# Conformer layer on eight cores: second half's normalized tokens transposed by DMA, W_out tiles re-placed in the down projection

## The reference

```
u = rms_norm(h, norm_mix_pre)
a_val, a_gate, q, k, v = split(u @ w_in)
conv_out = silu(layer_norm(depthwise_conv31(a_val * sigmoid(a_gate))))
attn_out = chunked_band_attention(q, k, v, rel_bias)
mixed = concat([conv_out, attn_out]) @ w_out
h = h + rms_norm(mixed, norm_mix_post)
u = rms_norm(h, norm_ffn_pre)
f = depthwise_conv3(u @ w_up);  gate, val = split(f)
h = h + rms_norm((gelu(gate) * val) @ w_down, norm_ffn_post)
```

## Time and profile before

| | |
|---|---|
| time, median of 3 runs (840.32 to 842.19) | 841.18 us |
| the profiled execution's own time | 841.79 us |
| its span on the slowest core | 840.7 us |
| spans of the eight cores | 834.7 to 840.7 us |
| mean granted TensorE clock of the cores | 0.987 to 0.996 of full speed |
| busy share of TensorE, VectorE, ScalarE, GpSimd | 94%, 70%, 59%, 21% |

### The profile page before, as it was taken

How to read it: one execution, slowest core, us unless ns; L and a number is a source line. 1 busy time by engine, 2 the same in 40 slices (tenths; PEclk the granted TensorE clock), 3 DMA queues, 4 the chain that set the end, 5 groups by cost and what they waited for, 6 DMA issues and landing times.

```text
span 840.7 us, 15580 instructions; the slowest of 8 cores (834.7 to 840.7 us)
## 1 busy us (share of the span) xinstructions
PE 790.6 (94%) x5324; PEld 420.1 (50%) x5324; DVE 588.2 (70%) x758; ACT 499.9 (59%) x764; POOL 179.7 (21%) x324
## 2 busy tenths in 40 slices
PE   1998998899998897999999999999999999999997
PEld 1545465554554445666666654444444444444443
DVE  2566477778757888889999984454488888885223
ACT  4567363525555787789888784323377777772111
POOL 3122121000003453232333311111222222200010
PEclk9999999999999999999999999999999999999999
DMA  8994778021637843599999995443398888811222
GB/s 258 310 292 133 126 151 101 27 44 9 127 92 129 166 157 102 60 101 107 111 113 114 181 147 159 153 161 139 126 153 78 78 76 80 77 15 50 102 101 101
DMA packets 145619, 101.00 MB, mean 120 GB/s; under 512 B 117122, under 2 KB 124674, under 8 KB 145156
## 3 DMA queue, kind: packets, MB, share of 16 engines
q0 software_dynamic: 95520, 31.37, 36.7%
q1 hardware_dynamic: 49444, 68.29, 27.8%
q10 hardware_dynamic: 576, 0.34, 0.1%
HBM read 110.31 MB, written 23.12 MB: 159 GB/s over the span
## 4 chain that ended last, share of the span: by engine, by line
PE 73%; DVE 13%; issue 7%; ACT 5%; DMA 1%; POOL 1%; DVEq 0%; ACTq 0%; POOLq 0%
PE ps L1277 24%; PE ps L1172 14%; PE ps L686 7%; PE ps L1088 5%; DVE big L1299 4%; DVE big L1302 4%; PE ps L672 3%; PE ps L599 3%; PE ps L658 3%; PE ps L920 2%; PE ps L790 2%; PE ps L826 2%; PE ps L615 1%; PE ps L1204 1%; PE ps L561 1%
## 5 line engine op out<-in xcount | busy, mean ns | idle before, releaser
L1277 PE MATMUL ps<-big 128*128 128x344 bf16 (+2 forms) x1760 | 310.9, 337 | 1.1 <-ACT big L1298 0.9
L1277 PEld LDWEIGHTS ps<-big 128*128 128x128 bf16 x1760 | 171.2, 98 | 139.8 <-issue 3.9
L1172 PE MATMUL ps<-big 128*128 128x512 bf16 x660 | 144.2, 378 | 0.0
L1299 DVE SCALAR_TENSOR_TENSOR big<-big 128x1026 f32<-128x1026 f32 (+1 forms) x88 | 113.0, 1285 | 20.3 <-ACT big L1289 11.2
L1163 POOL DMA_DIRECT2D big<-w_up x88 | 77.4, 880 | 213.0 <-PE ps L1277 192.4
L1302 DVE SCALAR_TENSOR_TENSOR big<-big 128x1026 f32<-128x1026 f32 (+1 forms) x88 | 113.3, 1288 | 9.4 <-DVE big L1299 0.7
L1294 ACT ACTIVATE big<-ps,big 128x1026 f32<-128x1026 f32 (+1 forms) x88 | 106.8, 1214 | 0.0
L1172 PEld LDWEIGHTS ps<-big 128*128 128x128 bf16 x660 | 63.7, 97 | 76.6
L801 ACT ACTIVATE big<-ps 128x1024 bf16<-128x1024 f32 x80 | 80.2, 1024 | 26.9 <-PE ps L790 22.3
L1088 PE MATMUL ps<-big 128*128 128x512 bf16 (+1 forms) x272 | 64.9, 391 | 2.1 <-DVE big L1036 2.1
L1290 ACT COPY big<-ps 128x1024 f32<-128x1024 f32 x44 | 44.6, 1015 | 36.1 <-PE ps L1277 36.0
(11 more groups left out here) (126 smaller groups left out, 934.2 us busy)
## 6 DMA issues: line engine op xcount, KB each, us to landing
big<-w_up POOLq DMA_DIRECT2D x88, 256.0 KB, 5.4
big<-xw SPq DMA_DIRECT2D x37, 512.0 KB, 6.6
big<-w_in SPq DMA_DIRECT2D x40, 256.0 KB, 12.3
h1s<-big SPq DMA_DIRECT2D x16, 512.0 KB, 2.9
big<-h1s SPq DMA_DIRECT2D x16, 512.0 KB, 5.1
out<-big SPq DMA_DIRECT2D x15, 512.0 KB, 2.9
big<-w_down POOLq DMA_DIRECT2D x22, 256.0 KB, 6.1
hd<-big SPq DMA_DIRECT2D x4, 512.0 KB, 3.4
```

The costliest lines, as they stand in the source:

```text
L1172: S.mm(lambda f=f, half=half, i=i: pe.matmul((PH[2] if i % 2 else PD).ap[:, half, :], lhsT=actb[f].ap[:, i * 128:(i + 1) * 128], rhs=Wd[f] ...
L1277: S.mm(lambda k=k, t=t, c0=c0, n_=n_: pe.matmul(pu.ap[:, t, 0:n_], lhsT=wb.ap[:, k, :], rhs=u2T.ap[:, k, c0:c0 + n_], start=(k == 0), stop ...
L1299: S.op("dve", lambda: dve.scalar_tensor_tensor(out=tbv, in0=xv[1], scalar=fdw.ap[:, cbk, 1:2], in1=tav, op0=ALU.mult, op1=ALU.add), reads= ...
```

## The change

For tiles 9 to 16 `wo_tp` no longer uses TensorE and ScalarE. The tile `ub5` is stored to a buffer in DRAM (`u5d`, 256 KB), and a second DMA from the SP queue, a transposing one (`dma_start_transpose`), reads it back into `u2q[t]`, laid out tile by tile as [8 channel blocks, 128 tokens]. Both are 8 instructions. The up projection of H = 1 reads its 512 columns as four runs of 128, one from each tile's buffer.

The down matmuls of each i are recorded in two equal pieces of 22, so there are 16 places p. The W_out tiles 9 to 16 go to the places `WPOS`, ahead of the piece there: two of three places for tiles 9 to 14, and the last two at places 9 and 10. `wo_u` and the store to `u5d` are recorded at the place after the tile's, the transposing DMA at the place after that. The eight `turns` are split over places 0 and 1.

A third edit is in `proj_a`: for group 4 and column blocks 0 and 1 (`pq`) the matmuls read their moving operand in the order q, s, that is 512 elements of 2 bytes with a step of 16 bytes, so that the sum lies in PSUM in that order and L694 reads both operands contiguously.

```diff
+WPOS = (0, 1, 3, 4, 6, 7, 9, 10)
...
+    u5d = nc.dram_tensor("u5d", [8, 128, D], BF16).ap()
...
+        u2q = [sb("u2q%d" % i, 16736 + i * 2048, [8, 128], BF16) for i in range(8)]
+        u2v = big[:, 16736 // 4:(16736 + 16384) // 4].bitcast(BF16).rearrange("p (t k m) -> p t k m", t=8, k=8)
...
+            pq = g == 4 and c < 2
             for k in range(8):
-                S.mm(lambda k=k: pe.matmul(b.ap[:, :n], lhsT=Wa.ap[:, k, col:col + 128], rhs=ut.ap[:, k, n0:N],
+                r_ = ut.ap[:, k, n0:N].rearrange("p (s q) -> p q s", q=8) if pq else ut.ap[:, k, n0:N]
+                S.mm(lambda k=k, r_=r_: pe.matmul(b.ap[:, :n].rearrange("p (q s) -> p q s", q=8) if pq else b.ap[:, :n],
+                                                  lhsT=Wa.ap[:, k, col:col + 128], rhs=r_,
...
-                    out=hs.ap[:, :, c, 0:s_], in0=sg.ap[:, :n].rearrange("p (s q) -> p q s", q=8), scalar=1.0,
-                    in1=b.ap[:, :n].rearrange("p (s q) -> p q s", q=8), op0=ALU.add, op1=ALU.mult),
+                    out=hs.ap[:, :, c, 0:s_], in0=v_(sg.ap[:, :n]), scalar=1.0,
+                    in1=v_(b.ap[:, :n]), op0=ALU.add, op1=ALU.mult),
...
-        def wo_tp(i):
+        def wo_tp(i, store=False):
...
+            if i > 8:
+                t = i - 9
+                if store:
+                    S.dma("sp", "u5w%d" % (t % 2), lambda: sp.dma_start(out=u5d[t], in_=u_.ap), reads=[u_], writes=[DH["u5%d" % t]], kb=256)
+                else:
+                    S.dma("sp", "u5t%d" % (t % 2), lambda: sp.dma_start_transpose(out=u2q[t].ap, in_=u5d[t]),
+                          reads=[DH["u5%d" % t]], writes=[u2q[t]], kb=768, desc=2)
+                return
...
+            pos = dict(zip(WPOS, range(9, 17)))
+            todo = []
+            for p in range(16):
+                i = p // 2
+                if p % 2 == 0:
                     if i:
+                        epi(i - 1)
+                    if i < 7:
+                        h1_in(i + 1)
+                if H == 0:
+                    if p in pos and pos[p] < 16:
+                        wo_x(pos[p] + 1)
+                    for p_, f in [x for x in todo if x[0] == p]:
+                        f()
+                    if p in pos:
+                        t = pos[p]
+                        wo_mm(t)
+                        wo_ev(t)
+                if H == 0 and p in pos:
+                    wo_res(t)
+                    wo_sq2(t)
+                    todo += [(p + 1, lambda t=t: wo_u(t)), (p + 1, lambda t=t: wo_tp(t, True)), (p + 2, lambda t=t: wo_tp(t))]
+                if H == 0 and p < 2:
+                    for f in turns[8 + 4 * p:12 + 4 * p]:
                         f[1]()
...
+                part(i, 11 * (p % 2), 11 * (p % 2) + 11)
...
-                need = [u2T[i_] for i_ in range(H, 9)]
+                need = u2q if H else [u2T[i_] for i_ in range(9)]
...
+                                                        rhs=u2T.ap[:, k, 342 * t:342 * t + n_] if not H else u2v[:, 4 * t:4 * t + 4, k, :],
```

More of the change, by code:

```diff
@@ L374, in build_program @@
         DH = {k: Buf(S, "dram", k, i, i + 1, None) for i, k in enumerate(
-            ["h1s", "wob"] + ["hd%d" % g for g in GS] + ["cd0", "cd1"])}
+            ["h1s", "wob"] + ["u5%d" % i for i in range(8)] + ["hd%d" % g for g in GS] + ["cd0", "cd1"])}
         pe, act, dve, pool, sp = nc.tensor, nc.scalar, nc.vector, nc.gpsimd, nc.sync
@@ L482, in build_program @@
         wo_h = [pb("woh0", 0), pb("woh1", 1)]
-        wo_t = pb("wot", 2)
         genpool = pb("genpool", 6, 2)
@@ L1136, in wo_u @@
                  reads=[h_, stat[r], g2b], writes=[u_], n=1024)
-        def wo_tp(i):
+        def wo_tp(i, store=False):
             n = np_of(i)
             u_ = wo_bufs(i)[2]
-            b = nbank() if i < 9 else wo_t
-            bb = (lambda: b.apb) if i < 9 else (lambda: b.ap.bitcast(BF16))
+            if i > 8:
[6 more added lines that the diff above has]
+                return
+            b = nbank()
+            bb = lambda: b.apb
             for k in range(8):
@@ L1229, in ffn_down @@
                 wo_x(9)
[L1230 to L1233, removed]
-                    if i:
[L1235 to L1246, removed]
+            pos = dict(zip(WPOS, range(9, 17)))
[3 more added lines that the diff above has]
+                if p % 2 == 0:
+                    if i:
+                        epi(i - 1)
[16 more added lines that the diff above has]
+                    for f in turns[8 + 4 * p:12 + 4 * p]:
                         f[1]()
                 if H and i == 7:
-                    last()
+                    if p % 2 == 0:
+                        last()
                     continue
[L1251 to L1260, removed]
+                part(i, 11 * (p % 2), 11 * (p % 2) + 11)
             if H == 0:
@@ L1272, in ffn @@
                 wb, pu = wring[si % NWR], PH[(si - 44) % 3] if H else PU[si % 2]
-                need = [u2T[i_] for i_ in range(H, 9)]
-                cols = [(342 * t, 342 if t == 2 else 344) for t in range(3)] if not H else [(2 + 512 * t, 512) for t in range(2)]
+                need = u2q if H else [u2T[i_] for i_ in range(9)]
+                cols = [342 if t == 2 else 344 for t in range(3)] if not H else [512] * 2
                 for k in range(8):
-                    for t, (c0, n_) in enumerate(cols):
-                        S.mm(lambda k=k, t=t, c0=c0, n_=n_: pe.matmul(pu.ap[:, t, 0:n_], lhsT=wb.ap[:, k, :],
-                                                        rhs=u2T.ap[:, k, c0:c0 + n_],
+                    for t, n_ in enumerate(cols):
+                        S.mm(lambda k=k, t=t, n_=n_: pe.matmul(pu.ap[:, t, 0:n_] if not H else pu.ap[:, t, :].rearrange("p (a b) -> p a b", a=4),
+                                                        lhsT=wb.ap[:, k, :],
+                                                        rhs=u2T.ap[:, k, 342 * t:342 * t + n_] if not H else u2v[:, 4 * t:4 * t + 4, k, :],
                                                         start=(k == 0), stop=(k == 7)),
```

1 line of the change is left out of this document (added).

## The result

The changed kernel took 860.75 us in the median of 4 runs, the kernel before 841.68 us beside it: a ratio of 1.023, with a 95% interval of 1.0204 to 1.0255. In some executions of either kernel the cores of one die run at a lower granted clock and take longer (one of these four took 996.07 us), and every ratio here leaves those out. The change is slower by 19 us where 6.4 us less was forecast.

A forecast was written before the change was run, and what follows sets the result against it. All three stages touched were taken as bound by TensorE. 7.7 us of turning removed less a new wait of 1.3 us gave 6.4 us, from the median 841.18 to 834.8 us, everything else at nothing; the range was 832.5 to 845.

The forecast's parts named there:

- the price of the strided operand: In proj_a, 32 matmuls reading a 2-byte element every 16 bytes: taken as nothing, at most 12.6 us; the least certain term.
- The lower end of its range: Whole kernel: 832.5 us, where the new wait does not appear and L694 gives its 0.4 us.
- Rival A: In proj_a the strided operand halves TensorE's pace: 6.9 us lost, 841.7 us, no change that can be told; chance 0.15.
- B: In proj_a the strided operand costs TensorE as much per column as VectorE, 12.6 us: 847.4 us, slower; chance 0.10.
- The down projection of H = 0: First W_out tile to the up projection of H = 1: 105 us instead of 111.5, 6.4 us gained.
- The wait ahead of tile 12: Down projection of H = 0: TensorE newly waits 1.3 us for L1102 to empty the PSUM bank.
- Tile 14: Down projection of H = 0: this W_out tile has 0.5 us to spare before TensorE would wait for its bank.
- the 2 us that the prediction named as a sign of being wrong: Down projection of H = 0: the prediction is wrong if TensorE's waits for VectorE grow past 2 us.
- all 7.7 us: Down projection of H = 0: turning costs TensorE 3.5 us of transposes and 4.2 us of waiting; all of it goes.
- The DMAs: Stores and transposing DMAs on SP: cost nothing; each transpose takes 6.2 us, the last tile landing 7 us ahead.
- The DMA share: Down projection of H = 0: 2 MB stored and 2 MB read raise it from 0.49 to 0.61 by bytes.
- The four runs of 128 columns: Up projection of H = 1: reading its columns so costs nothing, at most 1 us for the whole stage.

## Why the prediction was wrong

**The step that failed is the price of the strided operand.** The prediction took nothing for it, "because the nearest row is that of the same line on the same engine, contiguous", and set the upper end at what VectorE pays more per column, 0.77 ns. Measured is 1.76 ns per column in all, 1.33 more than contiguous; 32 matmuls cost 21.8 us. The surplus of one engine was the wrong thing to carry over, since it is counted from that engine's own pace. The time for one element would have come near, and the trace lets it be estimated twice. These are groups by line of the changed kernel, whose durations lie within 3 ns of those in the kernel before:

```profile
L1209 DVE TENSOR_TENSOR big<-big 128x1024 f32<-128x1024 f32 x15 | 18.4, 1227 | 2.6 <-DVE big L1206 2.6
```

```profile
L1106 ACT ACTIVATE big<-ps 128x512 bf16<-128x512 f32 x32 | 19.2, 599 | 17.2 <-PE ps L1095 7.2 <-DMA u5d<-big 6.2 <-PE ps L833 2.8
...
L1203 ACT ACTIVATE big<-ps 128x1024 bf16<-128x1024 f32 x15 | 15.3, 1020 | 79.2 <-PE ps L1187 79.1
...
L1041 ACT COPY big<-big 128x256 bf16<-128x256 bf16 x16 | 9.2, 640 | 0.0
```

VectorE takes 686 ns for 512 contiguous elements and 1227 for 1024, so some 145 ns go ahead; L694 with its 1079 ns thus takes an estimated 1.82 ns an element. ScalarE takes 599 and 1020 ns, 178 ahead; L1041, which reads single elements far apart, takes an estimated (640 - 178)/256 = 1.80 ns. These two are estimates, since the lines compared differ in operation and in what they read from PSUM; beside the measured 1.76 ns of TensorE they suggest that three engines of different pace pay much the same for an element that opens a line. With 1.80 ns the prediction would have had 32 x (0.92 - 0.22) = 22.4 us, and the right sign. (The lower end of its range plays no part, but its own terms give 834.8 - 1.3 - 0.4 = 833.1 us and not 832.5.)

Rival A had the mechanism and a third of the size, B was nearer, with 12.6 us. The Trainium skill's "Advanced Engine Details and Errata", section "SBUF Cachelines", is borne out in the 16-byte line. It asks for at least two hits on a line; if two are read as enough, that does not hold for TensorE here: two hits cost +0.25 us a matmul, four +0.015.

**A term was missing.** The same loop writes the down projection of H = 1, and the prediction costed the pieces of 11 for H = 0 alone. On the slowest core it costs 4.0 us: the wait of 2.19 us and, on this core, the clock behind it (below); on the five cores where the clock held it costs 2.3.

**The down projection of H = 0 was right in mechanism**, 106.2 us against a forecast of 105.1. The wait ahead of tile 12 was put at 1.3 us and is 1.59. It comes and goes with the landing of tile 9's rows of x: VectorE waits 2.58 us for them here, and on the slowest core of the run without the strided operand it waits for no load there and TensorE does not wait ahead of tile 12. Tile 14 was given 0.5 us to spare and waits 0.52. Together the waits are 2.11 us, just past the 2 us that the prediction named as a sign of being wrong. The prediction put all 7.7 us down to the turning on TensorE; with TensorE still turning the tiles, some 3 us of it went as well. What was missed is that ScalarE's first square of a tile (L1106) writes its unused result into the bf16 tile of two tiles earlier and so waits for the store of that tile, 6.2 us in all; that it costs TensorE anything is not shown. From 516 to 622 us, the waits of ScalarE (line, what it waited for, us in total, times, longest):

```profile
ACT big L1106 <- DMA u5d<-big: 6.2, 3, 2.9
```

**The DMAs were right in sum.** The groups of DMA issues of the changed kernel (the last number is the median in us from issue to landing), and its SP queue in order of time:

```profile
u5d<-big SPq DMA_DIRECT2D x8, 256.0 KB, 5.9
...
big<-u5d SPq DMA_TRANSPOSE x8, 4.9
```

```profile
609.60 1.81 SPq L1153 DMA_TRANSPOSE big<-u5d  x1
```

The transposing DMA lands in 4.9 us where 6.2 was taken, the store in 5.9 where a store of twice its size had taken 2.9. The last transpose is issued at 609.60 and, at the median time to landing (the eight took 3.4 to 7.2 us), lands 7.7 us ahead of the up projection (622.23); 7 was forecast. The DMA share is 0.70, not 0.61. With 4.9 us for eight blocks of 128x128, the price of 1309 ns a block in "VectorE: DVE Perf Modes" of the Trainium skill, section "The three transpose paths", is one that does not add up over a tile. **The four runs of 128 columns** cost nothing, as taken: 151.95 us for the stage, where it was 152.24.

## What to carry to other kernels

Ask of every operand that an engine reads with a step how many elements it uses of each 16-byte line, and price a line in nanoseconds of its own; where no row of that engine shows it, an engine that reads so gives an estimate. The faster the engine's own pace, the larger its surplus. An edit that eases an engine off the path is worth nothing that can be told even if it is free, and one that makes the bounding engine pay for it is a loss of its full price. When a loop serves two stages, cost the edit in both. And a chain through several engines needs room in the list of each: the same transposes cost TensorE 12.8 us of waits two places after their matmuls, and none four places after, once ScalarE no longer overwrote what they read.

## What the hardware showed that was not expected

The granted clock fell to 0.50, the lower of the two levels (1.2 GHz), while TensorE was busy without a gap: the strided matmuls brought it down, for without them it stays at 1.00 (the run without the strided operand), and it rose again once contiguous ones had followed. The strided ones did not feel it. Groups by line, first from 159.2 to 164 us, granted 1.00, then from 170 to 181 us, granted 0.50:

```profile
L691 PE MATMUL ps<-big 128*128 128x512 bf16 x6 | 5.6, 1078 | 0.0
```

```profile
L691 PE MATMUL ps<-big 128*128 128x512 bf16 x13 | 11.9, 1079 | 0.0
```

```profile
165.00:170.00 5.00, 5.00 (x21) 1.80 (x20) 2.44 (x2) 1.62 (x2) 0.20 (x1) 0.50 0.00 0
195.00:200.00 5.00, 5.00 (x53) 3.51 (x52) 2.55 (x7) 0.00 (x0) 0.24 (x1) 1.00 0.00 0
```

The work around them did: of the 10.58 us from 183.18 to 193.76, eight strided matmuls take 7.19, and the eight contiguous ones behind them 3.39 instead of 1.73. Such losses make up the 2 us of the stretch that the strided matmuls themselves do not explain.

A short wait can cost more than its length in the same way. After 2.19 us without work the clock of the stretch around it is 0.70 on the slowest core (busy times by stage):

```profile
780.00:785.00 5.00, 3.73 (x11) 1.48 (x12) 1.13 (x1) 0.00 (x0) 0.00 (x0) 0.70 0.02 3
```

From 781.27 to 844.70 us 286 matmuls take 63.43 us, where the kernel before took 66.53 us for 308, 0.216 each: 1.65 of the 4.0 us lost in the down projection of H = 1. But the fall does not always come. All eight cores of this execution wait 2.18 or 2.19 us there; on three the same matmuls then take 63.4 us, and on the other five 61.7 us, with the clock at 1.00 in the 8 us behind the wait. What decides is not shown.
